# Third weight block loaded ahead of the gating matrices and of two of x's tiles; the gating matrices' mask behind its low part

## What is computed

```python
xn = rms_norm(h, norm1_w[l])
proj = xn @ w_in[l] + b_in[l]
u, v, q, k, vg, r, g_lr, gate_a, gate_b = jnp.split(proj, split_points, axis=-1)
ya = chunked_sgu(jax.nn.gelu(u), jax.nn.gelu(v), sgu_ln_w[l], sgu_ln_b[l], sgu_w[l], sgu_b[l])
gk = jax.nn.log_sigmoid((g_lr @ w_gk2[l] + b_gk[l]).astype(jnp.float32)) / GLA_GATE_NORMALIZER
yb = gla(q, k, vg, gk, r, gla_norm_w[l])
merged = jax.nn.sigmoid(gate_a) * (ya @ w_branch_a[l]) + jax.nn.sigmoid(gate_b) * (yb @ w_branch_b[l])
h = h + merged @ w_out[l]
xn2 = rms_norm(h, norm2_w[l])
h = h + (jax.nn.silu(xn2 @ w_ffn_gate[l]) * (xn2 @ w_ffn_up[l])) @ w_ffn_down[l]
```

## Time and profile before

| | us |
|---|---|
| median of 3 runs | 819.62 |
| lowest, highest | 818.04, 819.68 |
| the profiled execution | 818.88 |
| its span, first to last instruction | 817.2 |
| PE busy in it | 808.4 (99%) |
| POOL, ACT, DVE busy | 413.1, 440.5, 535.7 |

### The profile page before, as it was taken

One profiled execution on the slowest core, in us unless ns is written; L12 is line 12 of the kernel. 1 busy time (PEld: TensorE's weight loads), 2 busy tenths in 40 slices (PEclk: granted clock), 3 DMA queues, 4 the chain that ended last, 5 costly groups with the idle time before them and its releaser, 6 DMA issues.

```text
span 817.2 us, 13355 instructions
## 1 busy us (share of the span) xinstructions
PE 808.4 (99%) x5500; PEld 749.6 (92%) x5500; DVE 535.7 (66%) x561; ACT 440.5 (54%) x502; POOL 413.1 (51%) x146
## 2 busy tenths in 40 slices
PE   8999999999999999999999999999999999999997
PEld 7788888888888899999998899999999999999985
DVE  5277277374774957888974278766667777677736
ACT  4533446756656645867442585444554446665624
POOL 3545425424224533477955443544444445878880
PEclk9999999999999999999999999999999999999999
DMA  8973422221133253322234202422234445436022
GB/s 334 222 250 128 155 103 79 76 103 52 52 104 105 102 206 105 103 103 105 85 131 201 103 1 103 144 107 107 108 108 159 161 156 190 173 123 216 1 78 103
DMA packets 27709, 103.11 MB, mean 126 GB/s; under 512 B 2832, under 2 KB 4496, under 8 KB 23696
## 3 DMA queue, kind: packets, MB, share of 16 engines
q1 hardware_dynamic: 22720, 88.12, 30.2%
q10 hardware_dynamic: 4944, 14.36, 5.7%
HBM read 94.08 MB, written 8.39 MB: 125 GB/s over the span
## 4 chain that ended last, share of the span: by engine, by line
PE 98%; DMA 0%; issue 0%; ACT 0%; SPq 0%; DVE 0%; ACTq 0%
PE acc L2118 14%; PE acc L2120 14%; PE acc L2121 14%; PE acc L1901 7%; PE acc L1903 6%; PE acc L1902 6%; PE acc L1918 6%; PE acc L1919 6%; PE acc L1920 6%; PE acc L2317 3%; PE acc L2316 3%; PE acc L2314 3%; PE acc L1949 3%; PE acc L2032 1%; PE acc L2071 1%; PE acc L2076 1%
## 5 line engine op out<-in xcount | busy, mean ns | idle before, releaser
L469 POOL TENSOR_TENSOR w_lo<-raw,w_hi 128x2048 fp32r<-128x2048 f32 x26 | 122.2, 4700 | 164.6 <-ACT w_hi L664 164.6
L490 POOL TENSOR_TENSOR A_lo<-wp,A_hi 128x1024 fp32r<-128x1024 f32 x51 | 126.0, 2470 | 144.7 <-ACT A_hi L840 137.4
L855 ACT ACTIVATE S_hi<-acc 128x1024 fp32r<-128x1024 f32 x68 | 68.1, 1024 | 89.5 <-PE acc L2121 56.3
L2120 PE MATMUL acc<-xt_lo,A_hi 128*128 128x256 f32 x408 | 115.5, 283 | 0.0
L2121 PE MATMUL acc<-xt_hi,A_lo 128*128 128x256 f32 x408 | 115.5, 283 | 0.0
L2118 PE MATMUL acc<-xt_hi,A_hi 128*128 128x256 f32 x408 | 115.5, 283 | 0.0
L1451 DVE TENSOR_TENSOR S_lo<-acc,S_hi 128x1024 fp32r<-128x1024 f32 x68 | 81.8, 1221 | 18.6 <-ACT S_hi L855 18.5
L1901 PE MATMUL acc<-xt_hi,w_hi 128*128 128x512 f32 (+1 forms) x240 | 92.5, 385 | 0.0
L1903 PE MATMUL acc<-xt_hi,w_lo 128*128 128x512 f32 (+1 forms) x240 | 91.7, 382 | 0.0
L1902 PE MATMUL acc<-xt_lo,w_hi 128*128 128x512 f32 (+1 forms) x240 | 91.7, 382 | 0.0
L664 ACT ACTIVATE w_hi<-raw 128x2048 fp32r<-128x2048 f32 x26 | 49.6, 1910 | 68.7 <-PE acc L1920 55.1
(11 more groups left out here) (325 smaller groups left out, 2333.4 us busy)
## 6 DMA issues: line engine op xcount, KB each, us to landing
wp<-wstream SPq DMA_DIRECT2D x34, 1024.0 KB, 7.0
raw<-wstream SPq DMA_DIRECT2D x26, 1024.0 KB, 4.9
wd<-wstream SPq DMA_DIRECT2D x16, 512.0 KB, 6.1
down_sums<-act_sum ACTq DMA_DIRECT2D x8, 512.0 KB, 3.2
sum_raw<-down_sums SPq DMA_DIRECT2D x8, 512.0 KB, 3.3
turned_sums<-tx ACTq DMA_DIRECT2D x4, 512.0 KB, 3.9
raw_out<-wstream SPq DMA_DIRECT2D x2, 1024.0 KB, 5.8
raw_ffn<-wstream SPq DMA_DIRECT2D x2, 1024.0 KB, 8.6
```

The source lines that it names most:

```text
L469: pool.tensor_tensor(w_lo[s][:, :], raw[s][:, :], w_hi[s][:, :], ALU.subtract).then_inc(lo_ready, 1)
L490: pool.tensor_tensor(low_of(name, rows), weights_of(name, c, rows), high_of(name, rows), ALU.subtract).then_inc(plain_low, 1)
L855: a.activation(high_of(name, rows), src, ACT.Copy).then_inc(op_high, 1)
L2120: pe.matmul(dst, wh[:, g, k, :], x[1][:, k, :], start=False, stop=False, skip_group_check=True)
```

## The change

SP's load of block 2 stands ahead of `swt` and of the two tiles of x, with the waits that the loop had for it. The load of block 3 stands behind them, with the loop's waits, and the loop begins with blocks 4 and 5. On POOL the low part of block 2 stands ahead of the mask, and that of block 3 behind it.

```diff
             for q in range(2, 4):
                 sp.dma_start(xw[:, 2 * q:2 * q + 2, :], x_t[:, 2 * q:2 * q + 2, :]).then_inc(xt_landed[q], 16)
+            sp.wait_ge(block0_low, 2)
+            sp.wait_ge(hi_ready, 1)
+            sp.wait_ge(lo_ready, 1)
+            sp.dma_start(raw[0][:, :], wstream[2]).then_inc(raw_landed[0], 16)
             sp.dma_start(swt[:, :, :], sgu_wt).then_inc(swt_landed, 16)
             for t in range(2):
                 sp.dma_start(xn_in[:, t, :], x[t * P:(t + 1) * P, :]).then_inc(x_landed[t], 16)
-            sp.wait_ge(block0_low, 2)
-
-            with sp.Fori(1, B_OUT // 2) as i:
+            sp.wait_ge(hi_ready, 2)
+            sp.wait_ge(lo_ready, 2)
+            sp.dma_start(raw[1][:, :], wstream[3]).then_inc(raw_landed[1], 16)
+
+            with sp.Fori(2, B_OUT // 2) as i:
...
             low(1, 1, 16)
+            low(2, 0, 32)
             pool.wait_ge(swt_landed, 16)

             pool.affine_select(out=swt[:, :, :], in_=swt[:, :, :], compare_op=ALU.is_ge, fill=0.0, base=0,
                                pattern=[[0, GROUPS], [1, P]], channel_multiplier=-1).then_inc(swt_masked, 1)
-            with pool.Fori(1, B_OUT // 2) as i:
+            low(3, 1, 32)
+            with pool.Fori(2, B_OUT // 2) as i:
```

## The result

The changed kernel took 820.21 us, median of 12 runs (819.26 to 823.42); the kernel before took 819.35 in the same comparison, median of 12 (817.68 to 819.70). The ratio is 1.002, 95% interval 1.0012 to 1.0028: slower by 0.2%, where 0.2% faster was forecast. Two later comparisons of the same pair gave 0.9999 (0.999 to 1.0008) and 1.0011 (0.9999 to 1.0022). The ratio is worked out over the runs and need not be the quotient of the two medians. So the change brought nothing and may cost some 0.2%. Of the changed kernel's 34 runs in the three comparisons 3 were under 818 us. Two executions of the whole study stand far outside, one of 2057 us (in *Only SP's order changed*) and one of 877 us (of before, second group); they are left out of the ratios.

The account below looks back on a forecast made before the run. PE, busy 99% of the span, was taken as the bound; removing its 1.62 us stall at block 2, all else costing 0, takes the median from 819.62 to 818.0 us, range 816.7 to 819.3.

Parts of the forecast that it names:

- The reading of the wait: PE at block 2's first matmul: stall worth 1.62 us, through the chain load, high part, low part, PE.
- The landing at 18.6: Block 2's load, issued at about 13.95, meets an empty queue and lands 4.6 us later; bounds 18.6 and 22.8.
- the low part's end: POOL's low part of block 2 ends between 25.2 and 25.7; PE wants it at 27.90.
- The mask and DVE's low parts: POOL's mask (1.54 us) moved behind block 2's low part, and DVE's low parts of x held by POOL: cost 0.
- The tiles of x: Two tiles go out later, through by 22.3; ACT's block 3 high part could start 0.7 us earlier; cost 0.
- Block 3's load and ACT's DMAs: ACT's two tiles and bias go out at 18.6 instead of 22.8 and compete with block 3's load; cost 0.
- The bound worked out there: From 16.1 us on, 5.8 MB of loads at 423 GB/s are all through at 29.8, wherever block 3 stands.
- Later supplies: Blocks 6 and 7: 0.26 and 0.41 us left if their chain doesn't move; it should come forward; cost 0.
- the second rival: The wait moves to blocks 6 and 7: block 3 lands at 29.8, 0.7 us of gain left, 818.9 us; 7%.
- strict order of the queues: Block 3's load: if the queues go in strict order, it lands at 25.2.
- The last rival: Slower: late tiles of x delay ACT's block 3 high part and so block 6; up to 0.6 us, 820.2; 5%.

Follow-up runs that it names:

- Only SP's order changed: Changed kernel, but on POOL the mask stays ahead of block 2's low part: 819.13 us, ratio 1.0003 to the kernel before.
- second group: Four experiments on the changed kernel, run on one chip with shared runs of the kernel before, which took 818.67 us there.
- all edits: Changed kernel; ACT's two small copies behind block 6's high part, bias, `swt` and mask later, ten or eight warm-up rounds: 817.49 and 817.70 (ten or unstated), 817.44 us (eight).
- ten rounds of warm-up: Changed kernel with ten rounds of warm-up matmuls instead of eight: 818.57 us, ratio 1.0003 to the kernel before.
- only the gating matrices later: Changed kernel with `swt` behind block 3's load and its mask behind block 3's low part: 819.66 us, ratio 1.0009 to the kernel before.

## Why the prediction was wrong

**What held.** The reading of the wait, 1.62 us at block 2, and its chain. The landing at 18.6 and the low part's end between 25.2 and 25.7 (with an early start the high part begins at 18.63 and the low part ends at 25.3). The mask and DVE's low parts at no cost (the last of these, number 7, ends at 28.02 with an early start and is wanted only by block 3). The tiles of x: the statistics of tiles 0 and 1 were done by 25.2, well ahead.

**The step that failed** is *Block 3's load and ACT's DMAs*, "Cost 0 for block 3", and with it the 0.7 us that *The tiles of x* and *Later supplies* let the chain come forward. The bound worked out there, all bytes through at 29.8, was right in kind and 1.0 to 1.5 us short (30.8 and 31.3 measured with an early start). I had the mechanism as the second rival, with its place, and gave it 7% and a gain of 0.7 us that was to be left; nothing was left, since the high part started at 31.38 and not at 29.8. I gave it so little because I measured the late landing against block 3's own use at 38.8 and let strict order of the queues be the likely case. The rows said otherwise already: two queues together carried 363 GB/s, so a megabyte issued 4 us sooner on ACT's queue had to come out of someone's share. The Trainium skill (DMA: Bandwidth & Descriptors, Queues, rings and completion order) says that an engine takes turns between the rings; the trace agrees where both queues have work, with 0.89 MB and 0.77 MB in the same four us and load and bias landing 0.2 us apart. The last rival's arithmetic then fits: it said slower from a high part at 30.5 on, and 31.38 gives 0.9 slower where the span showed 1.2. It only named the wrong late DMA, the tiles of x. (Its upper end is 0.7 us slower by its own figures, a high part from 31.2 on, where 0.6 was written.)

**A second step failed** without being written down: that the profiled execution stands for all. Its start was early. In 11 of 18 profiles PE comes to block 2 only at 29.4 to 31.1, and there is little or no wait at block 2 to remove. So the gain could only ever be had in part of the runs. How large that part is the profiles don't tell: in four experiments the profiled execution was the longest of its runs, and with all edits most timed runs lie at 817.2 to 817.8, where the profiles with an early start lie (817.41 and 817.64). Neither this nor the moved wait alone explains all of the first comparison: three of its runs were over 821.5, and I have no profile of such a run. That part stays open, and so does why the three comparisons gave 1.002, 0.9999 and 1.0011.

Sum for an early start, the second and third profile of the changed kernel against the first of before: 1.4 to 1.6 gained at block 2, 2.5 to 2.7 lost at block 6; block 6 begins 0.9 to 1.1 us later, and the span is 1.0 to 1.2 longer (818.2 and 818.3 against 817.2). For a late start: nothing gained, 0.3 lost at block 6 in the changed kernel's one profile of it.

## What to carry to other kernels

When a load is moved ahead, list every DMA that is issued behind an instruction which now runs earlier, on the other queues too, and ask which later load these will share the engines with, and whether they now go out ahead of it. A supply's margin is not its own use but the tightest use at the end of what is queued behind it: here block 3's high part could start 3.7 us later (32.3 against 28.6) for its own matmuls, and 0.3 us later by way of the statistics, a round trip through memory and block 6. And take more than one profile before you price a wait of 1.5 us near the start.

## What the runs showed of the hardware

- **The start scatters and carries the clock with it.** PE ended its warm-up at 4.6 to 5.8 us and stood for the first pieces of x and of the weights. In the late sort of start five to ten of the matmuls behind that wait came 0.427 us apart; 512 columns in 0.427 us is the lower of the two levels, 1.2 GHz. In two of the eleven (ten rounds of warm-up; only the gating matrices later) the windows show this level, 0.50 from 9 to 11 us; in the other nine they read 1.00 there, and the page's clock row shows 9s in all. So such a stretch is found by the starts. PE came to block 2 up to 3.2 us later with it, the wait for data included. When the first matmul came (5.5 to 6.6) did not tell the two sorts apart.
- **The port between DVE and POOL works both ways.** Before, a DVE instruction of 0.75 us took 4.66 behind POOL's; here POOL's of 4.6 us took 6.23 behind four of DVE's.
- **The same load of 1 MB, block 3, took from 4.7 to 10.9 us from issue to landing**: 10.3 and 10.9 in the changed kernel's early starts, with the bias issued ahead of it; 8.2 in its late start, with the bias behind it, and 7.3 to 8.2 with the bias moved away; 4.7 when it went out 7 us later, with nothing else left ahead of it.
